# Hybrid decoder layer: the low halves of three gate quarters are made elsewhere and at other times, and one quarter is loaded earlier

## What is computed

```python
ffn = _hierarchical_moe(x, rg_w, rg_b, re_w, re_b, e_gate, e_up, e_down)
x = _layer_norm(DEEPNORM_ALPHA * x + ffn, ln2_g, ln2_b)
return x + jax.nn.sigmoid(x @ ple_gate_w) * (p_i @ ple_proj_w)
```

## Time and profile before

| | us |
|---|---|
| median of 3 runs | 658.24 |
| lowest and highest run | 657.46, 658.48 |
| span of the profiled execution (first to last instruction) | 655.4 |
| TensorE busy in the span | 610.5 |
| VectorE busy in the span | 362.7 |
| GpSimd busy in the span | 167.1 |

### The profile page before, as it was taken

How to read it: one execution, slowest core, us unless ns; L and a number is a source line. 1 busy time by engine, 2 the same in 40 slices (tenths; PEclk the granted TensorE clock), 3 DMA queues, 4 the chain that set the end, 5 groups by cost and what they waited for, 6 DMA issues and landing times.

```text
span 655.4 us, 11779 instructions
## 1 busy us (share of the span) xinstructions
PE 610.5 (93%) x4597; PEld 442.2 (67%) x4597; DVE 362.7 (55%) x862; ACT 177.3 (27%) x351; POOL 167.1 (26%) x186
## 2 busy tenths in 40 slices
PE   7999999899999997999799999986699999978996
PEld 5868979677887886887675555554445565434885
DVE  6779999678969586768571123210111111119855
ACT  4673323334325233401101111111011111234321
POOL 2419181001001001331113333332323334110100
PEclk9999999899999998999899999997989999979999
DMA  6511432014002200197998999999999999949003
GB/s 237 212 55 57 169 121 105 1 33 162 0 1 83 111 0 10 56 356 303 368 368 305 415 416 415 419 417 419 413 422 417 415 417 417 405 162 358 1 1 131
DMA packets 29429, 150.27 MB, mean 229 GB/s; under 512 B 6520, under 2 KB 6800, under 8 KB 15416
## 3 DMA queue, kind: packets, MB, share of 16 engines
q1 hardware_dynamic: 23768, 141.04, 53.8%
q0 software_dynamic: 5600, 8.42, 3.5%
HBM read 145.62 MB, written 12.98 MB: 242 GB/s over the span
## 4 chain that ended last, share of the span: by engine, by line
PE 56%; DVE 13%; DMA 7%; issue 5%; ACT 1%; POOL 1%; SPq 1%; DVEq 0%; ACTq 0%
PE bank L2231 13%; PE bank L1868 7%; PE bank L1870 7%; PE bank L1869 7%; PE bank L2287 7%; DMA rows_x<-in_ple_gate_dram 4%; PE bank L2247 3%; DMA raw<-in_w_exp_dram 3%; PE bank L2221 2%; PE bank L2264 2%; PE bank L1991 1%; PE bank L1963 1%; DVE res L1342 1%; PE bank L1978 1%; PE bank L2181 1%
## 5 line engine op out<-in xcount | busy, mean ns | idle before, releaser
L1770 DVE COPY rows_x<-bank 128x128 f32<-128x128 f32 (+1 forms) x41 | 10.9, 267 | 181.9 <-PE bank L2279 100.8
L1868 PE MATMUL bank<-w_hi,a_hi 128*128 128x384 f32 (+1 forms) x240 | 88.7, 369 | 1.7 <-DVE a_lo L1524 1.7
L1870 PE MATMUL bank<-w_hi,a_lo 128*128 128x384 f32 (+1 forms) x240 | 86.9, 362 | 0.0
L1869 PE MATMUL bank<-w_lo,a_hi 128*128 128x384 f32 (+1 forms) x240 | 86.9, 362 | 0.0
L1868 PE MATMUL bank<-a_hi,w_hi 128*128 128x512 f32 (+1 forms) x176 | 69.4, 395 | 3.8 <-DVE a_lo L1524 1.5
L1869 PE MATMUL bank<-a_lo,w_hi 128*128 128x512 f32 (+1 forms) x176 | 67.7, 385 | 0.0
L1870 PE MATMUL bank<-a_hi,w_lo 128*128 128x512 f32 (+1 forms) x176 | 67.6, 384 | 0.0
L820 POOL DMA_INDIRECT pair_dram<-rows_x,row_put x26 | 26.4, 1014 | 105.4 <-ACT rows_x L1093 105.4
L1868 PEld LDWEIGHTS bank<-w_hi,a_hi 128*128 128x128 f32 x240 | 45.6, 190 | 7.1 <-DVE a_lo L1524 2.1
L2231 PE MATMUL bank<-raw,rows_x 128*64 128x256 f32 x416 | 47.7, 381 | 2.1 <-DMA raw<-in_w_exp_dram 1.6
L1869 PEld LDWEIGHTS bank<-w_lo,a_hi 128*128 128x128 f32 x240 | 45.5, 190 | 4.3
(11 more groups left out here) (304 smaller groups left out, 1118.5 us busy)
## 6 DMA issues: line engine op xcount, KB each, us to landing
raw<-in_w_exp_dram SPq DMA_DIRECT2D x45, 1024.0 KB, 20.5
slots<-in_w_exp_dram SPq DMA_DIRECT2D x24, 1024.0 KB, 22.9
pa<-in_w_exp_dram SPq DMA_DIRECT2D x21, 1024.0 KB, 19.3
raw<-in_w_in_dram SPq DMA_DIRECT2D x19, 512.0 KB, 3.9
raw<-in_w_wide_dram SPq DMA_DIRECT2D x4, 1536.0 KB, 7.2
raw<-in_w_out_dram SPq DMA_DIRECT2D x4, 1024.0 KB, 5.9
rows_x<-in_w_exp_dram SPq DMA_DIRECT2D x4, 1024.0 KB, 17.2
raw<-pair_dram SPq DMA_DIRECT2D x8, 512.0 KB, 9.6
```

Source lines behind the costliest of these rows:

```text
L1868: t_.matmul(o, lh, rh, start=first, stop=False)
L1869: t_.matmul(o, lh, rl, start=False, stop=False)
L1870: return t_.matmul(o, ll, rh, start=False, stop=last)
```

## The change

VectorE no longer subtracts quarters 2 and 3: GpSimd does, quarter 2 behind the inverse root of tile 0 and quarter 3 behind that of tile 1, counted by the semaphore `s_wlo`. VectorE subtracts quarter 1 behind the norm of tile 0 instead of ahead of it. For tile 1 its low halves of tile 0 come ahead of the first sum of tile 1 instead of behind it. SyncE issues quarter 3 behind the rows of tile 1 instead of behind those of tile 3. The waits of ScalarE and TensorE follow.

```diff
@@ SyncE @@
-                if t == 0:
-                    sp.dma_start(gate_raw[2], d["ple_gate"][2, :, :]).then_inc(s_quarter[2], 16)
-            sp.dma_start(gate_raw[3], d["ple_gate"][3, :, :]).then_inc(s_quarter[3], 16)
+                if t < 2:
+                    sp.dma_start(gate_raw[2 + t], d["ple_gate"][2 + t, :, :]).then_inc(s_quarter[2 + t], 16)
@@ GpSimd @@
             def rest():
+                def split_gate(q):
+                    pool.wait_ge(s_ghi, q + 1)
+                    pool.wait_ge(s_wlo, NPIECE + q - 2)
+                    g.tensor_tensor(gate_lo[q], gate_raw[q], gate_hi[q].bitcast(F32), ALU.subtract).then_inc(s_wlo, 1)
+
                 for t in range(NT):
                     inverse(t, s_ve2, s_rs2)
+                    if t < 2:
+                        split_gate(2 + t)
@@ ScalarE @@
-                act.wait_ge(s_glo, 2)
+                act.wait_ge(s_glo, 1)
@@ VectorE @@
                 split_gate(0)
-                split_gate(1)
                 for t in range(NT):
-                    expert_sum(t, 0)
+                    if t > 1:
+                        expert_sum(t, 0)
+                    if t == 1:
+                        dve.wait_ge(s_glo, 2)
                     if t:
                         turned_low(2 * t - 2, turned_2, s_x2hi, s_x2lo)
                         turned_low(2 * t - 1, turned_2, s_x2hi, s_x2lo)
+                    if t < 2:
+                        expert_sum(t, 0)
                     expert_sum(t, 1)
                     expert_variance(t)
...
                     norm_centre(t, s_ln2)
                     norm_scale(t, s_ln2, s_rs2)
                     if t == 0:
-                        split_gate(2)
-                    if t == 1:
-                        split_gate(3)
+                        split_gate(1)
@@ TensorE @@
-                    pe.wait_ge(s_glo, q + 1)
+                    pe.wait_ge(*((s_glo, q + 1) if q < 2 else (s_wlo, NPIECE + q - 1)))
```

## The result

The changed kernel took 667.72 us (median of 4 runs, 666.94 to 668.36), the kernel before beside it 658.36 (4 runs, 657.46 to 660.90): a ratio of 1.0144, 95% interval 1.0112 to 1.0176. It is slower, by 9.4 us. The profiled execution has a span of 666.6 and a time of its own of 668.36, so 1.76 us lie outside the span.

What follows compares the result with a forecast made beforehand. Bound: the tensor engine's unbroken stream, its start set by VectorE. 6.5 us to tile 1's transposes plus 1.5 for the clock make 8.0 on span 655.4, 663.4; plus 2.8 to the median: 666.2 us, range 662.0 to 667.6.

Steps and rivals of the forecast that it cites:

- first meeting: GpSimd's quarter 2 against VectorE's quarter 1, behind tile 0's norm: GpSimd goes first, first product 2.5 us later than before.
- The clock: Tensor engine's clock falls to 1.2 GHz behind gaps; paid only after the second, ahead of tile 1's transposes: 1.5 us (0 to 2.4).
- allowance of 0.5 us for scatter: In the range's lower end: the rivals' medians were taken to scatter by 0.5 us, like the runs shown.
- The bound: Tensor engine busy without break from 603.65 to 650.0 us; the kernel's end moves one for one with its start and stops.
- Quarter 1's subtraction leaves the front: Ahead of tile 0's sums on VectorE: first sum starts about 591.35 instead of 592.16, set by its rows; gain 0.8 us.
- Order behind the norm: Quarter 1 behind tile 0's norm, tile 1's sum behind the low halves: first product at 601.65, at most 2.0 us early.
- "GpSimd wins" at the norm: Behind tile 0's scale, waiting GpSimd gets in before VectorE's quarter 1, holds 598.7 to 603.3; winning both meetings had chance 0.67.
- rival 2: VectorE first at tile 0's norm, tile 1's sum and scale held: +5.3, to +6.8 with the clock, 663.5 to 665.0; chance 0.10.
- The second meeting: GpSimd's quarter 3 starts 0.1 us before tile 1's scale on VectorE and holds it: about 5.6 us instead of 1.28.
- The sum to the transposes: Total delay up to tile 1's transposes on the tensor engine: 618.45 in place of 611.95, +6.5 us.
- Free parts: Earlier load of quarter 3, ScalarE's weaker wait and the tensor engine's two changed semaphores: no time cost.
- From span to median: The 2.8 us by which the median 658.24 exceeds the span 655.4 is kept: 663.4 becomes 666.2.

Runs made afterwards that it cites:

- only_third: The kernel before, with quarter 3 alone subtracted by GpSimd behind the inverse root of tile 1, its load still last; ratio 1.0024.
- swap_halves: The kernel before, with tile 0's low halves ahead of tile 1's first sum and VectorE's quarter 3 subtracted in two halves; 657.26 us against 657.47.
- write_only: The changed kernel with GpSimd writing zeros instead of subtracting, reading nothing; low halves of quarters 2 and 3 left out of the computation; 657.37 us, ratio 0.9987.
- order_only: The changed kernel's order and loads, but VectorE does all subtractions, quarters 2 and 3 included; 659.90 us, ratio 1.0046 to the kernel before.
- side_by_side: The changed kernel with GpSimd subtractions paired with various VectorE instructions added behind its end; only the records count, its total time means nothing.
- changed_again: The changed kernel run once more, unaltered; 664.24 us, ratio 1.0113 to the kernel before.
- second_only: The changed kernel, but VectorE subtracts quarter 3 behind tile 1's scale and GpSimd has only quarter 2; 660.53 us, ratio 1.0049 to the kernel before.
- forced_first: The changed kernel with VectorE's subtraction of quarter 1 made to wait until GpSimd has subtracted quarter 2; ratio 1.0117 to the kernel before.
- filled_gap: The changed kernel with 30 useless filler products on the tensor engine ahead of tile 1's transposes; ratio 1.0151 to the kernel before.
- third_behind: The changed kernel, but GpSimd's subtraction of quarter 3 waits until tile 1's scale is done; ratio 1.0143 to the kernel before.

## Why the prediction came out as it did

It was right in the direction and in what decides it, and short in the size: 666.2 predicted, 662.0 to 667.6 as its range, 667.72 measured, 664.24 (5 runs) when the same kernel ran again. Three terms failed. The order of the first meeting came out the other way, which took the loss up to the transposes from 6.5 to 4.8 us. The clock, booked at 1.5, cost 2.45 in that order. And the allowance of 0.5 us for scatter was far too small: the start of the stage alone lies 3.95 us apart in the two profiles, and this, not the stage, puts the time above the forecast. When the kernel ran again, the median fell inside the range with the same errors in the sum; on which side of 667.6 it falls is luck. Step by step:

- *The bound.* Right: in every kernel above, the end moved with the tensor engine's stream. "Rest" is 42.46 to 42.83 wherever the clock stayed up behind quarter 3's first product, whatever happened earlier.
- *Quarter 1's subtraction leaves the front.* The rows set the first sum: it starts at t0 + 3.59 (predicted 591.35, t0 + 3.84), and the scale of tile 0 is 1.05 us earlier after t0, where 0.8 was booked. The number is right and the cause is not: with both subtractions still in front the sum starts at t0 + 3.55 in only_third and 3.61 in swap_halves. The late rounding in the one profile of before made the gain, and in such an execution as these two the edit gains nothing here.
- *Order behind the norm.* Predicted 2.0 us early at the first product, if nothing holds; 2.1 in the changed kernel, write_only and order_only. Of this 1.05 is the item above, and 1.06 the order: from the issue of tile 0's scale to the first product it is 4.27 us (14.03 − 9.76) in place of 5.33 (16.14 − 10.81).
- *"GpSimd wins" at the norm.* This is the step of the mechanism that failed in the profiled execution. The rule, that whoever waits goes in between two back-to-back instructions, holds (side_by_side). What was wrong was who waits: quarter 2 was taken to land as it did before, 0.5 us ahead of VectorE's turn; it landed later, GpSimd came 0.42 behind VectorE, and the first product was 4.6 us earlier than predicted. The meeting went as rival 2 has it there, with the sums of tile 1 held as rival 2 says (5.70 us for 2.67), as predicted in changed_again, and a third way in second_only and side_by_side. A step decided by half a microsecond of a transfer's landing deserved more than 0.10 for the other outcome.
- *The second meeting.* Right wherever GpSimd had quarter 3 and its early load: 5.44, 5.54, 5.53, 5.55 us (the last two in forced_first and filled_gap) for 5.6. The scale is issued 0.13 us behind GpSimd's subtraction in both profiles of the changed kernel; both hang on the same inverse root, and GpSimd is the engine that made it. The Trainium skill, SBUF — State Buffer, section "Who interferes with whom", describes these pairs, and the runs agree with it: two SBUF inputs on VectorE exclude a GpSimd instruction that reads SBUF and not one that only writes (5.02 us in side_by_side, 1.28 in write_only), and an operation with one input from PSUM isn't held (0.67). It also says that one-input operations such as a copy can exclude it in their fast two-port forms; the scaling and the copy of side_by_side, 4.48 us each, agree.
- *The sum to the transposes.* +6.5 predicted; +6.2 in the predicted order, +4.8 in the other. Rival 2 gave +5.3 for it.
- *The clock.* 1.5 predicted, from 0 to 2.4. Behind the stop of 6.7 us it cost 1.65 in the rest (44.31 − 42.66) and 0.80 in the transposes ahead of it (1.59 us to quarter 3 in place of 0.79), together 2.45, the upper end. In the predicted order it cost nothing: the prediction let the first gap's half clock fall into the second gap, but did not see that it thereby shortens the second gap to 1.68 us, behind which the clock stays up. (In the third order, in side_by_side, the second gap was 3.39 us and the granted clock fell to 0.50 from 621 to 623.) By its own order the sum is 6.0 of tail and not 8.0; by rival 2's it is 4.8 + 2.45 = 7.25. The two errors lie on opposite sides, so that 8.0 came near 7.25 partly by luck.
- *Free parts.* Booked at nothing, and no run says otherwise: the early load held nobody up, and a late one would have been rounded by about t0 + 20.7, ahead of the changed kernel's first use at t0 + 23.5.
- *From span to median.* The prediction kept the 2.8 us between the span and the median. 1.76 of it is start and end; the other 1.0 is that the profiled execution of before was a short one. From 666.2 to 667.72 it is + 3.95 (the later start of the stage), − 0.75 (7.25 for 8.0), − 1.04 (1.76 for 2.8) and − 0.64 (the median lies under the profiled 668.36). Of the 9.4 us of the first comparison some 7.25 to 8.3 belong to the stage. The range ended at 667.6, 0.12 below the measured median, because it had room for the stage's costs and only 0.5 us for scatter, while runs of one kernel lie up to 9 us apart. What makes t0 scatter was not looked into.

What stays open: the clock's share was read off the rows and not set by an experiment of its own, since filled_gap missed its case; and why quarter 2 lands now earlier, now later against t0 (its rounding starts between t0 + 7.56 in second_only and t0 + 9.38) was not settled.

## What to carry to other kernels

An idle GpSimd is not a free one. Before work is moved to it, ask of each VectorE instruction that will run at the same time whether it reads only SBUF; if so, and GpSimd's instruction reads SBUF too, it waits until that instruction ends, and what counts is which of VectorE's instructions that is. Here the same hold cost nothing on a sum with slack (a record of 5.58 us) and 4.2 us on the scale that TensorE waits for. Cutting or delaying the GpSimd work only moves the wait, as long as the result is wanted sooner than GpSimd can make it: with nothing held the move was still worth nothing (write_only). Before a gain is booked from one profile, look whether the wait that it removes is there in another: quarter 1's was not. And a stop of the tensor engine has a second price in the clock behind it, which depends on where the stop falls: 2.45 us behind one of 6.7 us, 1.4 behind one of 2.6 (third_behind), none behind one of 1.7.

## What was not expected of the hardware

- A one-input scaling and a copy, both SBUF to SBUF in float32, were held to the end of GpSimd's instruction like the two-input forms (4.48 us each for 1024 columns).
- Sixteen GpSimd subtractions of 128x128 took 9.68 to 12.21 us against 4.5 for one of 128x2048. The median piece took 0.45 to 0.46 us, so some 7.3 us are the pieces themselves (an estimate, 16 × 0.455), and the rest lies in longer records, up to 2.50 us, as they would be where VectorE had its turn.
- The granted clock fell to 0.50 behind stops of 5.0 and 6.7 us, and a stop of 2.55 us behind the transposes of third_behind was followed by 0.50 too, with a rest of 44.08. It stayed at 1.00 behind the stop of 1.7 us in changed_again, though a stretch at half clock lay not 10 us before it.
